# Sums of squares between the dense products, and one root for two norms

## The reference

```python
x = x + g1 * token_mixer(modulate(rms_norm(x, norm1_g), ...))     # ends in @ w_out
h = modulate(rms_norm(x, norm2_g), sh2, sc2)
x = x + g2 * conv_ffn(h, ...)                                     # w_up, 3x3 taps, silu * , w_down
x = rms_norm(x, final_g)                                          # "final1"
```

```python
h = concatenate([meta, x])
u = rms_norm(h, g_mix)                                            # "gmix"
z = u @ w_in_2                                                    # "proj2"
...                                                               # attentions, branch_a, branch_b
h = h + merged @ w_out_2                                          # "wout2"
h = h + expert_choice_ffn(rms_norm(h, g_ffn), ...)                # "gffn"
return rms_norm(h, g_final)[:, 16:]                               # "last"
```

## Time and profile before

| | us |
|---|---|
| median of 3 runs | 1435.86 (1435.27 to 1436.26) |
| the profiled execution | 1436.17 |
| its span | 1434.4 |
| PE busy | 1296.8 (90%) |
| DVE busy | 546.4 (38%) |
| ACT busy | 341.2 (24%) |
| POOL busy | 150.7 (11%) |
| dense products, L557 | 518.4 in 2096 records |
| sums of norms, L536 | 31.3 in 104 records |

### The profile page before, as it was taken

The page is one execution under the profiler, slowest core; times in us unless marked ns, Lnnn a source line. Parts: engine busy times, 40 slices in busy tenths (PEclk is TensorE's granted clock), DMA queues, the critical chain, the costliest instruction groups (busy, mean ns, idle before and its releaser), DMA issues.

```text
span 1434.4 us, 25888 instructions
## 1 busy us (share of the span) xinstructions
PE 1296.8 (90%) x11340; PEld 953.9 (67%) x11340; DVE 546.4 (38%) x1175; ACT 341.2 (24%) x879; POOL 150.7 (11%) x209
## 2 busy tenths in 40 slices
PE   5999829999997999999969999888899968999996
PEld 2744418989996788888858887556468755444433
DVE  1222454444336299993030541554424132001103
ACT  2211623343322132110011211333531022110101
POOL 0000047455410000121000000000000010000000
PEclk9999969999998999999989999999979978999999
DMA  9600001221115334344433334212103384999992
GB/s 401 262 0 0 30 29 62 92 91 62 63 62 235 118 117 176 125 155 141 145 138 118 118 118 142 94 59 70 48 2 118 118 331 180 398 428 427 428 426 106
DMA packets 18400, 223.60 MB, mean 156 GB/s; under 512 B 2096, under 2 KB 3120, under 8 KB 3824
## 3 DMA queue, kind: packets, MB, share of 16 engines
q1 hardware_dynamic: 17456, 219.27, 39.1%
q10 hardware_dynamic: 576, 1.63, 0.3%
q0 software_dynamic: 256, 1.06, 0.2%
HBM read 220.89 MB, written 1.05 MB: 155 GB/s over the span
## 4 chain that ended last, share of the span: by engine, by line
PE 86%; DVE 4%; ACT 4%; DMA 4%; POOL 1%; issue 1%; SPq 0%; DVEq 0%; ACTq 0%; POOLq 0%
PE ps L557 35%; PE ps L688 12%; PE ps L1040 7%; PE ps L862 5%; PE ps L910 4%; PE ps L1081 3%; PE ps L956 2%; PE ps L536 2%; DMA mem<-experts 2%; PE ps L1051 2%; PE ps L1021 2%; ACT mem L1315 1%; DMA mem<-consts 1%; PE ps L666 1%; PE ps L758 1%
## 5 line engine op out<-in xcount | busy, mean ns | idle before, releaser
L557 PE MATMUL ps<-mem 128*128 128x256 f32 (+2 forms) x2096 | 518.4, 407 | 18.5 <-DVE mem L1591 8.3
L557 PEld LDWEIGHTS ps<-mem 128*128 128x128 f32 x2096 | 402.1, 193 | 128.6 <-issue 47.9
L688 PE MATMUL ps<-mem 64*64 64x64 f32 (+1 forms) x5664 | 183.3, 222 | 27.5 <-POOL mem L1876 27.3
L688 PEld LDWEIGHTS ps<-mem 64*64 64x64 f32 x5664 | 177.2, 136 | 35.0 <-POOL mem L1876 28.0
L1620 DVE SCALAR_TENSOR_TENSOR mem<-ps,mem 128x189 f32<-128x189 f32 (+2 forms) x352 | 148.1, 431 | 16.0 <-ACT mem L1267 5.1
L1040 PE MATMUL ps<-mem 128*64 128x512 f32 x512 | 111.5, 592 | 1.1 <-DMA mem<-experts 0.6
L1040 PEld LDWEIGHTS ps<-mem 128*64 128x64 f32 x512 | 37.1, 137 | 73.7 <-issue 73.0
L1834 DVE TENSOR_TENSOR mem<-ps,mem 128x512 f32<-128x512 f32 x8 | 5.5, 692 | 187.4 <-PE ps L1040 187.4
L862 PE MATMUL ps<-mem 128*128 128x256 f32 x352 | 76.5, 379 | 0.0
L862 PEld LDWEIGHTS ps<-mem 128*128 128x128 f32 x352 | 66.6, 189 | 9.7
L910 PE MATMUL ps<-mem 128*128 128x272 f32 x256 | 63.2, 398 | 10.8 <-ACT mem L1343 10.8
(11 more groups left out here) (230 smaller groups left out, 1237.2 us busy)
## 6 DMA issues: line engine op xcount, KB each, us to landing
mem<-experts SPq DMA_DIRECT2D x48, 2048.0 KB, 17.7
mem<-weights SPq DMA_DIRECT2D x44, 2048.0 KB, 7.8
mem<-late_ada SPq DMA_DIRECT2D x16, 1024.0 KB, 5.0
mem<-weights SPq DMA_DIRECT2D x3, 1536.0 KB, 6.6
mem<-tokens SPq DMA_DIRECT2D x1, 2048.0 KB, 14.8
mem<-consts SPq DMA_DIRECT2D x1, 1633.0 KB, 18.9
out<-mem SPq DMA_DIRECT2D x1, 1024.0 KB, 4.8
mem<-consts POOLq DMA_DIRECT2D x1, 776.0 KB, 5.0
```

The costliest lines, as they stand in the source:

```text
L557: last = mm(bank(j % banks)[:, 0:nn], w[:, kc, c * P:(c + 1) * P], rr(kc), start=kc == 0, stop=kc == KD - 1)
L688: last = mm(out[hp, j], lhs[hp, j], rhs[hp, j], start=i == 0, stop=i == len(terms) - 1)
```

## The change

The sums of norm2 and gffn move between the products that feed them: after product j (j at least 1) TensorE sums the square of chunk j - 1, and the last sum stands behind the last product. In the last norm, four of the eight sums move between the groups of the last spread.

Between the blocks the two norms share one pass. Final1 gives h = x * g1 * r1 with r1 = rsqrt(M1 + eps), M1 the mean of x * x. The mean square of h is r1 * r1 * M2, with M2 the mean of (x * g1) squared, so gmix of h is x * g1 * g2 * rsqrt(M2 + eps * M1 + eps * eps). ScalarE squares each chunk of x twice, plain and with the gain g1; TensorE sums both (`final_sums`) between the groups of the down product, the first into bank 4, the second into bank 5 behind the 16 columns of the meta tokens' own sums (`meta_sums`). VectorE mixes the sums, ScalarE takes one root over 272 columns in two steps, and VectorE scales straight into `u`. Final1 itself is applied afterwards, for the residual `H`. The meta tokens' DMA is issued once `up` is done; the other two still come after a root. TensorE's wait for the three DMAs moves to the first rotation. Semaphores of three short sequences of VectorE become one.

```diff
-        NORMS = {"norm1": (0, 0), "four": (1, 8), "norm2": (2, 12), "final1": (3, 20), "gmix": (4, 28),
-                 "gffn": (5, 36), "last": (6, 44)}
+        NORMS = {"norm1": (0, 0), "four": (1, 8), "norm2": (2, 12), "gmix": (3, 20), "final1": (4, 20),
+                 "gffn": (5, 37), "last": (6, 45)}
+        META_SQUARES, FINAL_SQUARES = 21, 21
...
+            def norm_sum(name, sq, c, chunks, n, b):
+                pe.wait_ge(S("norm_squares"), NORMS[name][1] + c + 1)
+                last = mm(bank(b)[:, 0:n], cst("ones"), sq[:, c, 0:n], start=c == 0, stop=c == chunks - 1)
+                if c == chunks - 1:
+                    last.then_inc(S("norm_sums"), 1)
...
-                          wait_rhs=lambda kc: pe.wait_ge(S("rw_ready"), kc - NJ + 1) if kc >= NJ else None)
-            norm_sums("norm2", sq2, KD, TX, 7)
+                          wait_rhs=lambda kc: pe.wait_ge(S("rw_ready"), kc - NJ + 1) if kc >= NJ else None,
+                          after=lambda j: norm_sum("norm2", sq2, j - 1, KD, TX, 7) if j >= 1 else None)
+            norm_sum("norm2", sq2, KD - 1, KD, TX, 7)
...
+            def meta_sums():
+                pe.wait_ge(S("norm_squares"), META_SQUARES)
+                pe.wait_ge(S("down_taken"), 2)
+                for c in range(KD):
+                    mm(bank(5)[:, 0:META], cst("ones"), sq_meta[:, c, :], start=c == 0, stop=c == KD - 1)
+            def final_sums(c):
+                pe.wait_ge(S("norm_squares"), FINAL_SQUARES + 2 * c + 2)
+                one = mm(bank(4)[:, 0:TX], cst("ones"), sq2[:, c, :], start=c == 0, stop=c == KD - 1)
+                two = mm(bank(5)[:, META:L], cst("ones"), sq_gained[:, c, :], start=c == 0, stop=c == KD - 1)
...
-                    last.then_inc(S("down_read"), 1)
-            norm_sums("final1", sq2, KD, TX, 4)
-            pe.wait_ge(S("block2_in"), 48)
-            norm_sums("gmix", sqV, KD, L, 7)
+                        elif c == 3:
+                            last.then_inc(S("down_read"), 1)
+                        if half == 1 and q == 2 and c >= 1:
+                            final_sums(3 + c)
+                    if half == 1 and q == 0:
+                        meta_sums()
+                        final_sums(0)
+                        final_sums(1)
+                    if half == 1 and q == 1:
+                        final_sums(2)
+                        final_sums(3)
+            final_sums(7)
...
-            dense_product("wout2", lambda kc: ga[:, kc, :], L)
-            norm_sums("gffn", sqq8, KD, L, 7)
+            dense_product("wout2", lambda kc: ga[:, kc, :], L,
+                          after=lambda j: norm_sum("gffn", sqq8, j - 1, KD, L, 7) if j >= 1 else None)
+            norm_sum("gffn", sqq8, KD - 1, KD, L, 7)
...
+                    if i == NE // 2 - 1 and g >= 2:
+                        norm_sum("last", sqq8, 2 * g - 4, KD, TX, 0)
+                        norm_sum("last", sqq8, 2 * g - 3, KD, TX, 0)
...
-            norm("final1", xres, sq2, KD, TX, 4, root, EPS, wait=lambda c: act.wait_ge(S("down_taken"), c + 1))
-            norm("gmix", H, sqV, KD, L, 7, rt2, EPS,
-                 wait=lambda c: (act.wait_ge(S("H_ready"), c + 1), act.wait_ge(S("block2_in"), 48)))
+            act.wait_ge(S("block2_in"), 16)
+            A(sq_meta, H[:, :, 0:META], ACT.Square).then_inc(S("norm_squares"), 1)
+            for c in range(KD):
+                act.wait_ge(S("down_taken"), c + 1)
+                A(sq2[:, c, :], xres[:, c, :], ACT.Square).then_inc(S("norm_squares"), 1)
+                A(sq_gained[:, c, :], xres[:, c, :], ACT.Square, scale=prm("final_g", c)).then_inc(S("norm_squares"), 1)
+            act.wait_ge(S("mean_mixed"), 1)
+            A(rt2[:, 0:META], mean2[:, 0:META], ACT.Sqrt, scale=1.0 / D, bias=EPS)
+            A(rt2[:, META:L], mean2[:, META:L], ACT.Sqrt, scale=1.0 / D, bias=EPS * EPS).then_inc(S("norm_roots"), 1)
+            A(root[:, 0:TX], bank(4)[:, 0:TX], ACT.Sqrt, scale=1.0 / D, bias=EPS).then_inc(S("norm_roots"), 1)
...
+            tt(gain12, prm("final_g", 0, KD), prm("g_mix", 0, KD), ALU.mult)
...
+            dve.wait_ge(S("norm_sums"), NORMS["final1"][0] + 1)
+            own(V_.tensor_copy(mean2, bank(5)[:, 0:L]))
+            own.wait(dve)
+            stt(out=mean2[:, META:L], in0=bank(4)[:, 0:TX], scalar=EPS, in1=mean2[:, META:L], op0=ALU.mult,
+                op1=ALU.add).then_inc(S("mean_mixed"), 1)
+            dve.wait_ge(*norm_root("gmix"))
+            V_.reciprocal(rs2, rt2).then_inc(S("norm_recips"), 1)
+            dve.wait_ge(S("norm_recips"), NORMS["gmix"][0] + 1)
+            for c in range(KD):
+                stt(out=u[:, c, 0:META], in0=H[:, c, 0:META], scalar=prm("g_mix", c), in1=rs2[:, 0:META], op0=ALU.mult,
+                    op1=ALU.mult).then_inc(S("gmix_norm"), 1)
+                stt(out=u[:, c, META:L], in0=xres[:, c, :], scalar=gain12[:, c:c + 1], in1=rs2[:, META:L], op0=ALU.mult,
+                    op1=ALU.mult).then_inc(S("gmix_norm"), 1)
             apply_norm("final1", xres, H[:, :, META:L], TX, root, rstd, lambda c: prm("final_g", c), "H_ready")
-            apply_norm("gmix", H, u, L, rt2, rs2, lambda c: prm("g_mix", c), "gmix_norm")
...
-            pool.wait_ge(*norm_root("final1"))
+            pool.wait_ge(S("up"), 2 * NG)
             pool.dma_start(H[:, :, 0:META], dram["meta"]).then_inc(S("block2_in"), 16)
+            pool.wait_ge(*norm_root("gmix"))
             pool.dma_start(late, dram["consts2"]).then_inc(S("block2_in"), 16)
```

More of the change, by code:

```diff
@@ L245, in two_blocks @@
         ka_rest2 = whole.take(NJ)
+        gain12 = whole.take(KD)
         tokens = whole.take(KD, TB)
@@ L325, in two_blocks @@
         acc = mf.take(2, TX)
+        sq_gained = mf.take(KD, TX)
+        sq_meta = mf.take(KD, META)
         squares_f = spectrum.rearrange("p a b c -> p (a b c)")[:, 0:NJ * TX].rearrange("p (k t) -> p k t", k=NJ)
@@ L351, in two_blocks @@
         sined = [V[:, 0, 4 * i:4 * i + 3, :].rearrange("p a b -> p (a b)")[:, 0:L] for i in range(2)]
-        sqV = V.rearrange("p a b c -> p (a b c)")[:, 0:KD * L].rearrange("p (k t) -> p k t", k=KD)
+        mean2 = sqq[0]
         mx = Places(mem, arena - KD * TB, arena)
@@ L534, in norm_sums @@
                 for c in range(chunks):
-                    pe.wait_ge(S("norm_squares"), NORMS[name][1] + c + 1)
-                    last = mm(bank(b)[:, 0:n], cst("ones"), sq[:, c, 0:n], start=c == 0, stop=c == chunks - 1)
-                last.then_inc(S("norm_sums"), 1)
+                    norm_sum(name, sq, c, chunks, n, b)
+            def norm_sum(name, sq, c, chunks, n, b):
[3 more added lines that the diff above has]
+                    last.then_inc(S("norm_sums"), 1)
             def dense_product(name, rhs, n, wait_rhs=None, banks=4, width=None, wait_bank=None, after=None, end=None):
@@ L851, in _ @@
                           wait_bank=lambda e, j: e.wait_ge(S("ffn_taps"), 8 * (j + 1)))
+            def meta_sums():
[7 more added lines that the diff above has]
+                two = mm(bank(5)[:, META:L], cst("ones"), sq_gained[:, c, :], start=c == 0, stop=c == KD - 1)
+                if c == KD - 1:
+                    one.then_inc(S("norm_sums"), 1)
+                    two.then_inc(S("norm_sums"), 1)
             for half in range(2):
@@ L886, in rotate_heads @@
                         pe.wait_ge(S("qk_sined"), e - 1)
+                    if e == 0:
+                        pe.wait_ge(S("block2_in"), 48)
                     src = qb[:, e, :] if e < 8 else kb[:, e - 8, :]
@@ L899, in _ @@
             dense_product("proj2", lambda kc: u[:, kc, :], L, end=W_IN2 + 9,
-                          wait_rhs=lambda kc: pe.wait_ge(S("gmix_norm"), kc + 1), after=rotate_heads)
+                          wait_rhs=lambda kc: pe.wait_ge(S("gmix_norm"), 2 * kc + 2), after=rotate_heads)
             pe.wait_ge(S("proj2_taken"), 36)
@@ L1084, in _ @@
             spread(NE // 2 - 1)
-            norm_sums("last", sqq8, KD, TX, 0)
+            for c in range(4, KD):
+                norm_sum("last", sqq8, c, KD, TX, 0)
         def bc(ap, *shape):
@@ L1553, in _ @@
                         add(i, "R3", 0, ZT, Q, "R2_kept", d)
-            n = Tally(S("mix_steps"))
+            own = Tally(S("vector_steps"))
+            n = own
             n(tt(t4, iclr[:, 0, :, TC:TB], iclr[:, 1, :, TC:TB], ALU.add))
@@ L1589, in _ @@
             for j in range(NJ):
-                dve.wait_ge(S("mix_steps"), n.n - NJ + j + 1)
+                dve.wait_ge(S("vector_steps"), n.n - NJ + j + 1)
                 stt(out=y[:, 0, j, :], in0=y[:, 0, j, :], scalar=prm("gn_g", j), in1=y[:, 1, j, :], op0=ALU.mult,
@@ L1669, in _ @@
                 V_.tensor_copy(V[0:16, 2, e, :], bank(7)[0:16, 2 * P:3 * P]).then_inc(S("V_kept"), 1)
-            n = Tally(S("lam_steps"))
+            n = own
             dve.wait_ge(S("lam_exp"), 1)
@@ L1742, in _ @@
                 n(tt(ga[:, j, :], ga[:, j, :], gb[:, j, :], ALU.add))
```

(3 more changed lines are left out.)

## The result

| | before | changed |
|---|---|---|
| median of 4 executions, us | 1435.57 (1434.8 to 1436.26) | 1423.43 (1422.42 to 1423.94) |
| profiled execution: time, span | 1436.17, 1434.4 | 1423.18, 1421.3 |

The ratio is 0.9915, 95% interval [0.9898, 0.9932]: 12 us faster. Forecast were 3.2, and a range that ended 7 us above the result.

A forecast was written before the change was run, and what follows sets the result against it. TensorE, holding 86% of the chain, was taken to bound the kernel. Terms of -7.47, +0.75, +1.30 and +0.26 gave -5.16; clock terms +2.3 and -0.4 made -3.2: median 1432.7 us, range 1430.4 to 1435.4.

The forecast's parts named there:

- The clock: Step on TensorE's restarts at half clock: proj2 pays 2.3 us, shifted restarts give back 0.4, turning -5.16 into -3.2.
- the term -0.4 for the restarts that the change shifts: At up and branch_b: restarts charged near the top, drawn anew, give back 0.4 us, zero to 1.4 either way.
- norm2, add to root: In norm2, from the last add to the root takes 1.62 us; the sums moved between products cost 0.75 altogether.
- gffn, cost: At gffn, sums moved between products delay the last product and expose the table load: cost 1.30 us.
- last, cost: In the last norm, two sums ahead of the fourth spread group push its add: cost 0.26 us.
- last add to proj2: Between the blocks, TensorE starts proj2 6.7 us after VectorE's last add; with 7.10 added before, 13.80 against 21.27.
- price of proj2's restart: At proj2, restarting at half clock after a 4.4 us pause costs 2.3 us, the middle of 1.6 and 3.0.
- at full clock throughout: Whole kernel without clock effects: -7.47 between the blocks, +0.75 norm2, +1.30 gffn, +0.26 last, together -5.16 us.
- the clock stays up between the blocks: Rival: no clock fall in the pause before proj2, so -5.16 us and 1430.7; chance 0.18.
- the clock takes more: Rival: proj2 pays 3.0 us and other restarts give nothing back: -2.2, 1433.7, up to 1435.4; chance 0.20.
- The table stall: Rival: table switches stall past their load, 1.38 us each at gffn and last, 0.6 between blocks: 1436.1; chance 0.03.
- A sum between products: Rival at 23 places in wout, wout2, down, last spread: each costs 0.4 us extra, +6.0, 1441.9; slower had 0.04.

The follow-up runs named there:

- a_pad2: The changed kernel with two repeated matmuls (0.9 us of work) in proj2, just ahead of the attentions: median 1431.84 us, ratio 0.9964.
- a_pad4: The changed kernel with four repeated matmuls (1.8 us of work) in proj2, just ahead of the attentions: median 1432.69 us, ratio 0.9984.
- again: The changed kernel executed once more, unaltered: median 1424.84 us (1421.8 to 1431.1, 6 executions), ratio 0.9936.
- the filled kernels: Kernels with twelve unread matmuls at the attentions' end: before 1428.69 us, changed 1426.53, between-blocks part 1420.85, interleaving 1431.75; with more pauses filled, 1412.03 against 1419.83.
- b_tail: The kernel before with twelve unread matmuls in TensorE's pauses at the end of the attentions: median 1428.69 us, ratio 0.9965.
- b_all: The kernel before with unread matmuls ahead of wout, after norm2's sums, between the blocks, in attentions, at branch_b, after gffn's sums: 1419.83 us, ratio 0.9897.

## Why the prediction was wrong

The step that failed is the one under "The clock", and in it the term -0.4 for the restarts that the change shifts ("drawn anew I expect 0.4 back from the two, zero to 1.4 either way"), with which the range was built. It was put at -0.4 and measured -10.5. Everything else in the sum came out:

| step | predicted | measured |
|---|---|---|
| norm2, add to root | 1.62 | 1.72 |
| gffn, cost | 1.30 | 1.31 (wout2's start to the router: chains 15.08 apart, then 13.77) |
| last, cost | 0.26 | 0.2 (spread's start to root: 7.22 before, 7.39 after) |
| sums of the meta tokens | 1.89 | 1.85 |
| start of down to the last add, longer by | +7.10 | +6.87 (76.40 to 83.27) |
| last add to proj2 | 6.70 | 6.71 |
| pause of TensorE, clock falls in it | 4.4 | 4.2; it fell |
| price of proj2's restart | 2.3 | 2.3 |
| other pauses and restarts | -0.4 | -10.5 |

The last row is 1.5 at wout (its stage and norm2's took 0.7 less, where the schedule added 0.8), 1.4 at up (155.80 to 154.43), 5.8 in the attentions, 2.5 in branch_b's first product (6.42 to 3.93), less 0.7 from the router to the experts. With the schedule's -5.4 as measured, proj2's 2.3, and 0.6 by which the first constants came later in that execution, that makes 13.0 of the 13.1 between the spans. Of the last row, the 1.5 and 1.4 at wout and up are in part luck of the execution that was profiled: the kernel before itself took either price, as shown under the stages. The prediction also calls its -5.16 "at full clock throughout", which it isn't: the 21.27 of before hold the 1.6 that gmix's sums lost at half clock.

Two mistakes are in it. I listed the restarts that follow a clean pause, three rows of the chain, and did not look at the clock in the windows of the attentions. There TensorE does not stand still for more than 1.4 us at a time (the rows below), and yet its clock fell for 20.5 us. Two such pauses lie close together, and of the 4.7 us before the fall (1037.8 to 1042.5) it worked 1.8. The pattern of pauses does not decide it alone: in the changed kernel the same records stand behind the same pauses, 1.39 us at 1030.89 and 1.41 at 1033.01, and its clock came back after 3.4 us. And I gave a fall a price of at most 3.0. The price of one after which the clock stays low for 20.5 us is well above that: 5.8 + 2.5 = 8.3 here, and 7 to 9 in a_pad2 and a_pad4. The timeline of the kernel before around that fall, with the pauses in brackets:

```profile
...
1039.18 0.71 PE L941 MATMUL ps<-mem 16*128 16x16 f32 x6 [1.39 <-DVE mem L1716]
1041.31 0.85 PE L941 MATMUL ps<-mem 128*128 128x128 f32 x6 [1.41 <-ACT mem L1331]
1041.99 6.05 PE L956 MATMUL ps<-mem 128*128 128x272 f32 x12
```

Are these places drawn at random, or does the schedule fix them? Four profiles are of kernels with the same proj2 restart. From its first matmul, the granted clock of the next 6 us is, in the changed kernel, again, a_pad2 and a_pad4:

```profile
...
738.38:744.38 6.00, 6.00 (x16) 4.64 (x17) 5.96 (x16) 0.00 (x0) 0.00 (x0) 0.61 0.47 154
```

```profile
...
737.66:743.66 6.00, 6.00 (x16) 4.64 (x17) 5.96 (x16) 0.00 (x0) 0.00 (x0) 0.61 0.45 162
```

```profile
...
737.81:743.81 6.00, 6.00 (x16) 4.63 (x17) 5.96 (x16) 0.00 (x0) 0.00 (x0) 0.60 0.45 160
```

```profile
...
737.50:743.50 6.00, 6.00 (x16) 4.63 (x17) 5.96 (x16) 0.00 (x0) 0.00 (x0) 0.61 0.48 163
```

The clock came back 4.7 to 4.8 us after the restart each time (6 us at a mean of 0.61 are 4.7 at half), that is at about 743.1, 742.4, 742.6 and 742.2 of the four spans. So at proj2 the clock stood alike against the work in all four. Behind that they part, and not only where work was added. `again` is the changed kernel unaltered, yet its profile has half clock from 1022.2 to 1032.5 and from 1035.9 to 1039.3 where the other has 3.4 us from 1033.2, and its branch_b starts 4.0 us later behind the restart of proj2:

```profile
...
1026.00:1030.00 4.00, 4.00 (x8) 2.25 (x9) 0.00 (x0) 1.21 (x5) 0.00 (x0) 0.50 0.00 0
```

So the schedule does not fix the place, and a restart alone does not either. What holds is the count of executions: 0.9 to 1.8 us of added work took the changed kernel from one in ten above 1431 to 14 in 16. What inside the chip decides a single execution was not tried and stays open.

Of the rivals, "the clock stays up between the blocks" is refuted by these rows, and "the clock takes more" by the price of 2.3 and the restarts that became cheaper. The table stall is refuted by gffn, where the root starts 0.02 us after the end of the load of 1142.57. The Trainium skill's page "ScalarE: Activation LUTs", What ACT_TABLE_LOAD costs, adds a drain of 1.38 us to a load: if there is one, it isn't paid behind the load here. A sum between products costs itself only: in down the sums at 728.00 and 728.43 are followed by the next product at 728.86, in the changed kernel.

So the 13.1 us between the two profiled executions are 5.4 of the schedule, less 2.3 at proj2's restart, and 10.5 of TensorE's clock elsewhere, of which 2.9 (wout, up) come and go in one and the same program. For the medians the split is less sharp: the schedule's part is 5.2 by the sum (7.47 less 2.3 for the three norms) and 2 to 5 by the filled kernels (7.8 less 3.1 to 5.7). The whole change with all pauses filled was not run, so this part was never measured by itself. Open stays why nine of ten executions of the changed kernel are under 1427 and only 4 of 84 of the kernel before under 1428: profiles show one execution each. Interleaving cost more in the filled kernels (3.1 and 5.7) than the 2.3 of the sum, which I put down to falls of the clock that the twelve matmuls leave, without a run that shows it.

## What to carry to other kernels

Where a change moves work in time and the bound engine has a clock that falls in its pauses, go through the granted clock of the whole profile first and list every stretch at half clock, above all those with work in them: they can be worth more than the change, and they move with any displacement. Then a few matmuls that nobody reads, put in the pauses, can make such a stretch shorter or go away and the comparison of two schedules cleaner; look at the profile again, since twelve of them left the changed kernel 2.7 us slower. Here 57 of them were worth 15 us on one and the same schedule (1427.35 to 1412.03). And sums put between products take nothing off the engine that does both; behind the last product they were the cover for the add, the square and the table load.

## What the runs showed of the hardware that was not expected

- TensorE at 1.2 GHz for 20.5 us while it was busy 88 to 100% of each window of 4 us (before, 1044 to 1060), with no pause in the trace longer than 1.4 us ahead of it. In the 4.7 us before the fall it had worked 1.8.
- Added matmuls made kernels faster: 12 of them 6 us (before to b_tail), 68 of them 15 us (before to b_all). The same 12 made the changed kernel 2.7 us slower.
- One program's executions spread over 16 us (84 of the kernel before), of which the mean granted clock of each shows a part: in one job the fastest (1424.8) had 0.968 and the slowest (1438.7) 0.954.
- Two profiles of the changed kernel, the first with 3.4 us and `again` with 13.7 us at half clock in the attentions, had the same clock against the work at proj2's restart.
